# A spare tile of 192 bytes ahead of the GEMM inputs: where a matmul's moving operand starts in SBUF

## The reference, cut to what matters

```
z = h @ w_in[l]                                  # 1024 x 7424
merged @ w_out[l]                                # 1024 x 1024
causal_dwconv(h @ w_up[l], ...)                  # 1024 x 5632
(jax.nn.silu(h @ w1) * (h @ w3)) @ w2            # 1024 x 2816 twice, 2816 x 1024; four times
u = h @ w_in; wq, wkv, wo, conv_pw, attn_o ...   # second block, per layer
```

## The kernel before, in words

| tile | start | modulo 8192 | modulo 512 |
|---|---|---|---|
| raw_weights | 16512 | 128 | 128 |
| weights_hi | 41088 | 128 | 128 |
| weights_lo | 57472 | 128 | 128 |
| x_res, y, squares | 73856, 82048, 90240 | 128 | 128 |
| ones, flip, headsum | 113120 and on | | 480 |
| h_hi | 115392 | 704 | 192 |
| h_lo | 123584 | 704 | 192 |
| gh, hidh, mh | 131776 | 704 | 192 |
| hidl | 154304 | 6848 | 192 |
| xq, xk, xv | 148160, 156352, 164544 | 704 | 192 |

## Time and profile before

### The profile page before, as it was taken

How to read it: one execution, slowest core, us unless ns; L and a number is a source line. 1 busy time by engine, 2 the same in 40 slices (tenths; PEclk the granted TensorE clock), 3 DMA queues, 4 the chain that set the end, 5 groups by cost and what they waited for, 6 DMA issues and landing times.

```text
span 2466.6 us, 43523 instructions
## 1 busy us (share of the span) xinstructions
PE 2333.6 (95%) x17913; PEld 2229.1 (90%) x17913; DVE 1697.7 (69%) x2655; ACT 1199.9 (49%) x1803; POOL 88.0 (4%) x78
## 2 busy tenths in 40 slices
PE   6998898999999999999999999999999999999997
PEld 5976898999999997889898999999997889898997
DVE  5666886887664797877655664664897887555663
ACT  2565445664544534454535444444534455535443
POOL 1000000110010000000000110010000000000110
PEclk9998999999999999999999999999999999999998
DMA  8534575558565553346444655665562346444652
GB/s 248 163 118 131 171 237 162 183 168 260 171 184 184 176 179 95 113 127 191 141 147 124 189 179 159 183 184 182 178 184 87 111 136 189 140 143 136 182 183 82
DMA packets 397941, 400.89 MB, mean 163 GB/s; under 512 B 18006, under 2 KB 391112, under 8 KB 397745
## 3 DMA queue, kind: packets, MB, share of 16 engines
q1 hardware_dynamic: 395361, 389.27, 51.6%
q0 software_dynamic: 2384, 8.85, 1.1%
HBM read 396.98 MB, written 1.09 MB: 161 GB/s over the span
## 4 chain that ended last, share of the span: by engine, by line
PE 76%; DVE 15%; ACT 5%; issue 3%; DMA 1%; DVEq 0%; POOL 0%; ACTq 0%; POOLq 0%
PE gemm_ps L862 62%; DVE weights_lo L1453 4%; PE gemm_ps L865 4%; DVE y L1901 3%; PE misc_ps L1002 2%; PE misc_ps L1003 2%; PE misc_ps L946 2%; PE misc_ps L955 1%; DVE mod_partial L1550 1%; ACT weights_hi L1128 1%; ACT e L1251 1%; PE misc_ps L1035 1%; DVE y L1601 1%; PE misc_ps L999 1%; PE misc_ps L1020 1%
## 5 line engine op out<-in xcount | busy, mean ns | idle before, releaser
L1453 DVE TENSOR_TENSOR weights_lo<-raw_weights,weights_hi 128x1024 fp32r<-128x1024 f32 x704 | 837.2, 1200 | 451.6 <-ACT weights_hi L1128 449.7
L862 PE MATMUL gemm_ps<-h_hi,weights_hi 128*128 128x256 f32 x3536 | 1012.2, 286 | 44.0 <-DVE h_lo L1587 28.1
L1128 ACT CAST weights_hi<-raw_weights 128x1024 fp32r<-128x1024 f32 x704 | 719.3, 1033 | 681.2 <-PE gemm_ps L862 619.8
L862 PE MATMUL gemm_ps<-h_lo,weights_hi 128*128 128x256 f32 x3536 | 999.0, 283 | 0.0
L862 PE MATMUL gemm_ps<-h_hi,weights_lo 128*128 128x256 f32 x3536 | 997.4, 282 | 0.0
L862 PEld LDWEIGHTS gemm_ps<-h_hi,weights_hi 128*128 128x128 f32 x3536 | 675.7, 191 | 53.1 <-issue 48.9
L862 PEld LDWEIGHTS gemm_ps<-h_lo,weights_hi 128*128 128x128 f32 x3536 | 675.8, 191 | 3.7 <-issue 3.0
L862 PEld LDWEIGHTS gemm_ps<-h_hi,weights_lo 128*128 128x128 f32 x3536 | 673.6, 191 | 0.0
L862 PE MATMUL gemm_ps<-hidh,weights_hi 128*128 128x256 f32 x880 | 247.8, 282 | 1.5 <-DVE weights_lo L1453 1.5
L862 PE MATMUL gemm_ps<-hidl,weights_hi 128*128 128x256 f32 x880 | 246.0, 280 | 0.0
L862 PE MATMUL gemm_ps<-hidh,weights_lo 128*128 128x256 f32 x880 | 245.6, 279 | 0.0
(11 more groups left out here) (284 smaller groups left out, 2660.6 us busy)
## 6 DMA issues: line engine op xcount, KB each, us to landing
raw_weights<-in_ffn_w_dram SPq DMA_DIRECT2D x256, 512.0 KB, 3.8
raw_weights<-in_w_in_dram SPq DMA_DIRECT2D x200, 512.0 KB, 3.7
raw_weights<-in_w_mod_dram SPq DMA_DIRECT2D x48, 512.0 KB, 4.9
raw_weights<-in_w_up_dram SPq DMA_DIRECT2D x44, 512.0 KB, 4.6
raw_weights<-in_xattn_kv_dram SPq DMA_DIRECT2D x32, 512.0 KB, 4.4
raw_weights<-in_w_out_dram SPq DMA_DIRECT2D x24, 512.0 KB, 4.5
raw_weights<-in_w_down_dram SPq DMA_DIRECT2D x20, 512.0 KB, 4.8
raw_weights<-in_w_branch_dram SPq DMA_DIRECT2D x16, 512.0 KB, 4.6
```

The costliest lines, as they stand in the source:

```text
L862: mm = pe.matmul(ps[:, c, 0:T], w[:, m, kt, c * P:(c + 1) * P], x[:, f, :], start=start, stop=stop_)
L1128: act.copy(unit_of(WH, m % SPLIT, u), unit_of(RAWB, u["raw"] % RAW, u)).then_inc(sems["weights_rounded"], 1)
L1453: dve.tensor_tensor(unit_of(WL, m % SPLIT, u), unit_of(RAWB, u["raw"] % RAW, u), unit_of(WH, m % SPLIT, u), ALU.subtract).then_inc(sems["w ...
```

## The change

One tile of 48 float32, 192 bytes of a partition, is asked for ahead of `h_hi`. Nothing reads or writes it. Everything asked for behind it starts 192 bytes later: `h_hi`, `h_lo` and all tiles of all stages. What stands ahead of it (`raw_weights`, both weight tiles, `x_res`, `y`, `squares`, the norms' rows, `ones`) stays.

More of the change, by code:

```diff
@@ L594, in build @@
     NM, DEN, RD, ES = sb("neg_max", [P, 4]), sb("den", [P, 4]), sb("rden", [P, 4]), sb("sink_exp", [P, 4])
+    sb("spacing", [P, 48])
     HH, HL = sb("h_hi", [P, NF, T], F32R), sb("h_lo", [P, NF, T], F32R)
```

## The result

The changed kernel takes 2495.88 us (median of 4 runs, 2494.17 to 2496.98) against 2467.99 us for the kernel before on the same chip: a ratio of 1.0114, interval 1.0102 to 1.0127. It is 28 us slower.

What follows compares the result with a forecast made beforehand. The prediction took GEMM matmuls one behind the other on PE to bound the kernel, 1606 of 2466.6 us. Removed work 0, added work 0 and unchanged pitch times 13600 gave 0 us: 2467.7 us forecast, range 2400 to 2535.

Steps and rivals of the forecast that it cites:

- The leverage: GEMM matmuls on the chain: 1 ns of pitch times 13600 matmuls is worth 13.6 us, 0.55% of the run.
- The likeliest case: Whole run: pitch unchanged, small drift included, 2467.7 us with its own range 2464 to 2472; chance 0.50.
- the rival on the slower side: GEMM matmuls: at 256 apart moving reads meet the load's once more, pitch 122.1 ns, 2526 to 2538 us; chance 0.15.
- Pitch unchanged times 13600: 0 us: GEMM matmuls on the chain: the moved addresses leave the pitch of 117.8 ns as it is, costing 0 us.
- the second reading: GEMM pitch, some 10 ns above streaming: the excess goes with columns moved, not with the stationary load running beside.
- The third reading: Form F and L865: operand starts don't matter, since opposite-sign distances both give 5.66 us for a pair of 48.
- The first reading: GEMM pitch: other engines' traffic doesn't cause the excess, 117.6 ns with them idle against 117.8 busy.
- point of decision: GEMM matmuls: the slower rival decides once the pitch is above 118.2 ns, 0.4 ns times 13600 being 5 us, 0.2%.
- The drift of the share at the faster pace: GEMM matmul pairs: a changed share at the faster pace, 0.21 us per pair, stays within 0.2%; counted within the 0.50.
- The far rival on the faster side: GEMM matmuls: all collisions go, pitch falls to 107.8 ns, 136 us gained, 2332 us; faster by much more had chance 0.10.

Runs made afterwards that it cites:

- e10: Changed kernel (distance 256) with form F matmuls loading and using only 64 of each block's 128 weight columns: 2419.43 us, ratio 0.9813 to the kernel before.
- e6_d192: Changed kernel with a spare tile of 128 bytes ahead of h_hi, distance of moving and stationary operand 192: 2447.98 us, ratio 0.9919 to the kernel before.
- e1: Kernel before with the 192 bytes ahead of raw_weights, so every tile moves and the distance stays 64: 2467.15 us, ratio 1.0003.
- e2_d0: Changed kernel with a spare tile of 448 bytes ahead of h_hi, distance of inputs and weights 0: 2495.39 us, ratio 1.0125 to the kernel before.

## Why the prediction came out as it did

*The leverage was right.* I put 1 ns of pitch at 13.6 us, on 13600 matmuls of the chain. The measured 2.2 ns (120.0 less 117.8) give 30 us by that; the run lost 28. That the order, DVE, ACT and the plain products would stay held as well: their times are within 0.2% of before.

*The likeliest case was wrong.* The measured 2495.88 us lies within the range of 2400 to 2535, but only because the range takes in the rival on the slower side, which had a chance of 0.15; the forecast of 2467.7 us and its own range of 2464 to 2472 missed by 28 and 24 us. "Pitch unchanged times 13600: 0 us" is the step that failed, and what failed in it is the second reading, that the excess goes with the columns moved and that the load beside has no part in it. In the earlier trace rows 512 columns have 233.3 ns and 256 have 117.8, 1.98 times as much for twice the columns, with one load each: excesses of 20.0 and 11.1 ns, but from one layout, in which form F has the distance 64 and the matmuls that move 512 columns have 192. At 256 they are 13.3 ns (120.0 less 106.7) and, for most of the 512-column ones, 13.3 as well (226.6 less 213.3; 15.4 over all of them): the same sum for one load, whatever is moved. The pitch at 256 columns rose and the one at 512 fell, which an excess that goes with the columns alone doesn't do. e10 points to the load as the cause: half of its columns took 6.7 ns off each pitch (120.0 to 113.3). The ratio of about two belongs to the distances of before: in e6_d192, where the matmuls that move weights have 64, the excesses are 10.4 and 16.3 ns, a ratio of 1.6. I took one layout's ratio for a law.

*The third reading was half right.* Starts do nothing by themselves, as e1 shows. But I took L865 and form F as two different distances with one pace, and concluded that distance didn't matter, where it was a chance: 64 and 192 share the pace of 5.66 us for a pair, and in the means they differ, 117.6 and 116.2 ns. I had both pairs in the earlier trace rows and the mean over all of L865 was there to be asked for.

*The first reading held.* With the other engines nearly idle the pitch is 120.0, as with them busy.

*The rival on the other side was the right one,* "slower by one step": the moving reads meet the load's once more. That it came out so is in part luck, for nothing in the rows of before said which way a distance of 256 would go. Its place, its sign and its point of decision held (120.0 ns against 118.2, and 152.63 us for the piece against 150.3); its size was taken from the only step that the trace shows, 4.3 ns, and is 2.2 ns. At 13600 matmuls that is the difference between 2526 us and the measured 2496. The drift of the share at the faster pace, which I held for small, is small here (4.5% of form F's pitches before, 0.2% after), but it is what makes 192 fast. The far rival on the faster side, a pitch of 107.8, comes from reading a plain record as two passes, which no run shows, and has a row against it that the prediction didn't look for: the few GEMM matmuls that move only 128 columns stand 111.6 ns apart before, although 128 columns are 53.3 ns by the estimate above, which suggests that with a full load for each matmul 107.8 ns was out of reach.

*What stays open.* Why 0 and 96 are slow and 32 and 192 not; what makes a stretch take the faster or the slower pace at one distance; why the halved load gives so little at 64; and how much of the gain at 256 would come from the halved result alone. That the reads meet in SBUF is the reading that fits a period in addresses; what is shown is the distance, its period at the distances that were run, and that halving the load with its result counts.

## What to carry to other kernels

In this kernel, where TensorE streams float32r matmuls one behind the other with a new stationary operand for each, the place of the moving operand relative to the stationary one modulo 256 bytes is worth 2% of the run: 2448 us at 192, 2468 at 64, 2496 at 0, 96 or 256. It changes with every tile between weights and inputs whose size isn't a multiple of 256 bytes, however small, so a change that only adds a tile is to be measured against a version with the same distance. Try the multiples of 32 that the allocator allows, and expect a difference of a few tenths of a per cent from run to run at the best ones (2449.37 to 2462.02 us over the 10 runs at 448).

When an excess is to be put down to one of two things that always come together, here the columns moved and the loads, two points from one layout don't separate them. Halving the loads alone, with the columns moved left as they were, nearly did; it left the halved result as the one thing that changed along with them.

## What the runs showed of the hardware

- The pitch of a float32r matmul with 256 moving columns, as the mean of 48 successive ones where the granted clock was 1.00, went by the distance: 119.6 to 120.0 ns in every such stretch of after (distance 256) and e2_d0 (0); 117.8 in 218 of the 223 of before (64), and 113.3 to 113.7 in the other 5; 117.8 in 152 of the 220 of e6_d192 (192), and 113.3 to 113.8 in 68. With halved loads at 256 (e10_half_load_d256) it was 113.4 in 208 of 217.
- Where the granted clock was 0.50 the same matmul had 213.3 to 213.5 ns in before, after, e2_d0, e6_d192 and e10_half_load_d256, at distances of 64, 256, 0, 192 and 256, the last with halved loads.
- The plain float32 products of L946 kept their 215.6 ns per record in before and after (3.45 us for 16).
- At distance 256 (after) 111 of the 174 pitches of 512-column matmuls have a mean of 226.6 ns, 106.6 above the 120.0 of the 256-column ones: 0.42 ns for each further column.
- At distance 0 and 256 the excess over the estimated 106.7 ns for 256 columns is 13.3 ns with a load of 128 columns (120.0), and at 256 it is some 6.7 with one of 64 columns (113.3), there with half the result left out too. A load of 128 float32 columns reads 512 bytes of a partition, so that is an estimated 2.6 ns for each 100 bytes.
- The 44 pitches of matmuls that move 128 columns at the full clock have a mean of 111.6 ns before and 111.7 after, far above half of the 117.6 and 119.9 ns of 256 columns.
- The faster pace at 64 and 192, 113.4 ns with a full load, is the same as with the halved load at 256: an excess of 6.7 ns.
- VectorE's and ScalarE's times did not follow this move of their operands by 192 bytes: 1697.1 and 1198.4 us busy after the move, 1697.7 and 1199.9 before.
